# First attention of a two-block transformer kernel: the window branch's projection, key rotation and key spreading, and the compressed keys' rotation, at other units

## The reference, cut to what matters

```python
h = x @ w_in_even[li]
qa, ka, va, qn, kc, vc, ksl, vsl, kw, vw, g = _split(h, EVEN_SPLITS)
...
kc = partial_rope(compress(k_cmp, 0), cmp_end)   # branch 1: 15 compressed keys per group
...
ks = partial_rope(k_slc, pos)                    # branch 2: selected keys
...
kw_pad = jnp.pad(partial_rope(k_win, pos), ...)  # branch 3: window keys
...
return gb[..., 0:1] * o_c + gb[..., 1:2] * o_s + gb[..., 2:3] * o_w
```

## Time and profile before

| | |
|---|---|
| median of 3 runs | 1347.26 us (1346.98 to 1348.11) |
| the profiled execution | 1347.95 us |
| its span in the profile | 1346.2 us |
| TensorE busy | 1319.9 us, 98% of the span |
| VectorE busy | 681.1 us, 51% |
| ScalarE, GpSimd busy | 234.5 us and 95.6 us |
| mean granted TensorE clock | 0.997 of full speed |

### The profile page before, as it was taken

The page is one execution under the profiler, slowest core; times in us unless marked ns, Lnnn a source line. Parts: engine busy times, 40 slices in busy tenths (PEclk is TensorE's granted clock), DMA queues, the critical chain, the costliest instruction groups (busy, mean ns, idle before and its releaser), DMA issues.

```text
span 1346.2 us, 19454 instructions
## 1 busy us (share of the span) xinstructions
PE 1319.9 (98%) x7520; PEld 821.7 (61%) x7520; DVE 681.1 (51%) x1263; ACT 234.5 (17%) x547; POOL 95.6 (7%) x116
## 2 busy tenths in 40 slices
PE   9999999999999999999999999999999999999996
PEld 8667585786779557587687666644444444444433
DVE  1235588877889548977978254422122122212213
ACT  2134311111120341120122252100000000000002
POOL 1125400000011030000000100000000000000001
PEclk9999999999999999999999999999999999999999
DMA  9930154555514455577664504499999999999994
GB/s 380 360 142 34 64 220 177 219 228 218 185 67 157 183 194 201 217 270 280 233 240 168 187 34 186 180 420 421 421 420 416 422 421 421 422 421 421 421 420 194
DMA packets 51072, 359.56 MB, mean 267 GB/s; under 512 B 5920, under 2 KB 6192, under 8 KB 8496
## 3 DMA queue, kind: packets, MB, share of 16 engines
q1 hardware_dynamic: 45312, 324.60, 59.8%
q0 software_dynamic: 5392, 32.05, 6.5%
q10 hardware_dynamic: 288, 1.80, 0.3%
HBM read 356.88 MB, written 1.05 MB: 266 GB/s over the span
## 4 chain that ended last, share of the span: by engine, by line
PE 88%; DVE 8%; issue 1%; DMA 1%; ACT 0%; DVEq 0%; SPq 0%; ACTq 0%
PE ps L1536 13%; PE ps L1010 13%; PE ps L1001 9%; PE ps L1565 7%; PE ps L1461 7%; PE ps L1514 7%; PE ps L983 5%; PE ps L818 4%; PE ps L1291 4%; PE ps L901 2%; PE ps L1284 2%; PE ps L922 2%; DVE ring L2381 1%; DMA ring<-in_stream 1%; PE ps L823 1%
## 5 line engine op out<-in xcount | busy, mean ns | idle before, releaser
L2829 DVE TENSOR_TENSOR masked_and_probs<-ps,gate_rows 128x512 f32<-128x512 f32 x52 | 33.5, 686 | 152.4 <-PE ps L1565 152.4
L1514 PE MATMUL ps<-masked_and_probs,probT 128*128 128x512 f32 x208 | 94.4, 594 | 1.0 <-DVE masked_and_probs L2829 1.0
L1461 PE MATMUL ps<-masked_and_probs,mix_rows 128*128 128x256 f32 (+1 forms) x416 | 93.0, 376 | 0.0
L1461 PEld LDWEIGHTS ps<-masked_and_probs,mix_rows 128*128 128x128 f32 x416 | 75.0, 190 | 28.8 <-issue 19.6
L1001 PEld LDWEIGHTS ps<-xT,ring 128*128 128x128 f32 x768 | 87.8, 192 | 3.8 <-issue 3.8
L1001 PE MATMUL ps<-xT,ring 128*128 128x128 f32 x768 | 88.7, 275 | 0.0
L1010 PE MATMUL ps<-ring,qk_tiles 128*128 128x512 f32 x192 | 85.2, 592 | 0.0
L983 PE MATMUL ps<-ring,xT 128*128 128x512 f32 x192 | 83.8, 594 | 0.0
L2817 DVE TENSOR_TENSOR masked_and_probs<-masked_and_probs,ps 128x256 f32<-128x256 f32 x26 | 11.0, 421 | 142.0 <-ACT masked_and_probs L2003 142.0
L1673 ACT ACTIVATE qk_tiles<-ps 128x512 f32<-128x512 f32 (+7 forms) x58 | 30.1, 522 | 244.9 <-PE ps L1001 237.2
L1536 PE MATMUL ps<-ring,vec_rows 128*32 128x512 f32 (+2 forms) x296 | 72.0, 592 | 0.0
(11 more groups left out here) (500 smaller groups left out, 2379.9 us busy)
## 6 DMA issues: line engine op xcount, KB each, us to landing
ring<-in_stream SPq DMA_DIRECT2D x200, 1024.0 KB, 9.8
qk_tiles<-in_stream SPq DMA_DIRECT2D x46, 1024.0 KB, 20.0
v_rows<-in_ada POOLq DMA_DIRECT2D x12, 1024.0 KB, 5.2
qk_tiles<-in_ada POOLq DMA_DIRECT2D x12, 1024.0 KB, 5.2
vec_rows<-in_stream SPq DMA_DIRECT2D x12, 1024.0 KB, 17.0
con<-in_stream SPq DMA_DIRECT2D x12, 1024.0 KB, 18.6
y_rows<-in_stream SPq DMA_DIRECT2D x12, 1024.0 KB, 20.1
par<-in_stream SPq DMA_DIRECT2D x12, 1024.0 KB, 20.7
```

The lines of the kernel that those rows point to most:

```text
L1461: mm = pe.matmul(ps[:, 5 + kk // 2, kk % 2 * 2 * P:kk % 2 * 2 * P + width], h2[:, t, k * P:(k + 1) * P], select[:, t, 0:width], start=t == ...
L1514: mm = pe.matmul(ps[:, q, :], probT[:, buf, 256 + q // 2 * P:256 + (q // 2 + 1) * P], yslot[:, q % 2 * 512:(q % 2 + 1) * 512], start=False ...
L2829: dve.tensor_tensor(yslot[:, cols], ps[:, 5 + half, :], gaterow[:, 1, cols], ALU.mult).then_inc(ready, 1)
```

## The change

It moves work between units and reorders GpSimd's first steps; no instruction of work is added or removed.

- Compressed keys: TensorE's rotation from 4 to 3 (ahead of the query piece there), VectorE's from 5 to 4. The second half of the query pieces from 6, 7, 8, 9 to 5, 6, 7, 8.
- Queries: ScalarE's second copy from 10 to 9; VectorE's sine parts from 10 and 15 to 9 and 13.
- Branch 3: pieces from 14 to 19, 21, 22 to 11 to 18; ScalarE's copy from 23 to 19; VectorE's rotation from 27 to 24; spreading from 28 and 30 to 26 and 27.
- GpSimd: `spread_values` first, then a new wait for `s_ckey` 2, then `cosine_part(0)`.

```diff
--- before.py
+++ after.py
@@ -239,8 +239,8 @@
 
 
 STARTING = 4
-KEYS_AT = 5
-ROPE_AT = (10, 15)
+KEYS_AT = 4
+ROPE_AT = (9, 13)
 
 
 def by_scalar(u):
@@ -1230,12 +1230,12 @@
             pe.wait_ge(s_roped, 2)
             attention("a0", {
                 0: [compressed, lambda: queries(0, 0, 0)], 1: [lambda: queries(0, 0, 1)],
-                2: [lambda: queries(0, 1, 0), lambda: pe.wait_ge(s_projsb, 4)], 3: [lambda: queries(0, 1, 1)],
-                4: [rotate_compressed], 6: [lambda: queries(1, 0, 0)], 7: [lambda: queries(1, 0, 1)],
-                8: [lambda: queries(1, 1, 0)], 9: [lambda: queries(1, 1, 1)],
-                14: [lambda: window_keys(0)], 15: [lambda: window_keys(2)], 16: [lambda: window_keys(4)],
-                17: [lambda: window_keys(6)], 18: [lambda: window_values(0, 0)], 19: [lambda: window_values(0, 4)],
-                21: [lambda: window_values(1, 0)], 22: [lambda: window_values(1, 4)],
+                2: [lambda: queries(0, 1, 0), lambda: pe.wait_ge(s_projsb, 4)], 3: [rotate_compressed, lambda: queries(0, 1, 1)],
+                5: [lambda: queries(1, 0, 0)], 6: [lambda: queries(1, 0, 1)], 7: [lambda: queries(1, 1, 0)],
+                8: [lambda: queries(1, 1, 1)],
+                11: [lambda: window_keys(0)], 12: [lambda: window_keys(2)], 13: [lambda: window_keys(4)],
+                14: [lambda: window_keys(6)], 15: [lambda: window_values(0, 0)], 16: [lambda: window_values(0, 4)],
+                17: [lambda: window_values(1, 0)], 18: [lambda: window_values(1, 4)],
                 CMP_AT: [compressed_scores], CMP_AT + 8: [turn_compressed],
                 CMP_AT + 10: [lambda: compressed_sums(0)], CMP_AT + 11: [lambda: compressed_sums(1)]})
             out_projection(FIRST["out_even"], "mix0", lambda: turn_rows(x, "ln0", 0))
@@ -1839,10 +1839,10 @@
                 a, b = INSTANCES[name]
                 return {b - a + 1: lambda: take_turn(name.replace("a", "mix"), xT, only=0)}
 
-            exps("a0", {2: take_compressed, 4: lambda: take_queries(0), 10: lambda: take_queries(1), 23: take_window,
+            exps("a0", {2: take_compressed, 4: lambda: take_queries(0), 9: lambda: take_queries(1), 19: take_window,
                         24: exp_compressed, CMP_AT + 9: take_compressed_turn,
                         CMP_AT + 11: lambda: take_compressed_sums(0), CMP_AT + 12: lambda: take_compressed_sums(1)} | {
-                (5, 7, 28, 30)[2 * j + g]: (lambda j=j, g=g: spread_keys(j, g)) for j in range(2) for g in range(2)}
+                (5, 7, 26, 27)[2 * j + g]: (lambda j=j, g=g: spread_keys(j, g)) for j in range(2) for g in range(2)}
                 | turn_first_half("a0"))
             warm()
             take_turn("mix0", xT, only=1)
@@ -2164,7 +2164,7 @@
                     dve.tensor_scalar(drms, drms, -0.5, None, ALU.mult)
                     dve.tensor_scalar(drs.bitcast(I32), dnw.bitcast(I32), -1, ROOT_SEED, ALU.mult, ALU.add).then_inc(s_drs, 1)
 
-                return {DIFF_NORM_AT[0]: lambda: sums(0), DIFF_NORM_AT[1]: lambda: (sums(1), rope_keys(1)), DIFF_NORM_AT[1] + 1: first_guess}
+                return {DIFF_NORM_AT[0]: lambda: sums(0), DIFF_NORM_AT[1]: lambda: sums(1), DIFF_NORM_AT[1] + 1: first_guess}
 
             def branch_gates():
                 dve.wait_ge(s_expgate, 1)
@@ -2565,7 +2565,7 @@
 
             attention("a0", {2: branch_gates, KEYS_AT: rope_compressed, ROPE_AT[0]: lambda: rotated_queries(0),
                              ROPE_AT[1]: lambda: rotated_queries(1), CMP_AT + 1: compressed_masked, CMP_AT + 2: compressed_max,
-                             CMP_AT + 3: compressed_less_max, CMP_AT + 5: compressed_factors,
+                             CMP_AT + 3: compressed_less_max, CMP_AT + 4: lambda: rope_keys(1), CMP_AT + 5: compressed_factors,
                              CMP_AT + 6: compressed_weighed} | norm_diff() | turn_first_half("a0"))
             take_turn("mix0", xT, only=1)
             residual("out_even", 0, lambda t: layer_norm(t, vec[:, 0, :], vec[:, 2, :], s_vecA, 32), "ln0", 0)
@@ -3092,8 +3092,9 @@
                                    own[0:8 * NCMP, :].unsqueeze(2).to_broadcast([8 * NCMP, 8, HD]), ALU.mult
                                    ).then_inc(s_vspread, 1)
 
+            spread_values()
+            pool.wait_ge(s_ckey, 2)
             cosine_part(0)
-            spread_values()
             scale_group(0)
             roped_queries(0)
             cosine_part(1)
```

## The result

| | kernel before, run beside it | changed kernel |
|---|---|---|
| median of 22 runs | 1348.09 us (1346.93 to 1350.85) | 1350.55 us (1347.62 to 1352.22) |
| ratio of the two, 95% interval | | 1.0015 (1.0009 to 1.0020) |
| the profiled execution, its span | 1347.95, 1346.2 us | 1350.91, 1349.2 us |
| mean granted clock over the runs | 0.9969 (0.995 to 0.999), of the 35 beside e1 to e5 | 0.9936 (0.991 to 0.995) |

The change makes the kernel slower by about 0.15%, some 2 us. That is within the 0.2% called "no change" above, but a ratio of 1.0015 on 1347.26 is 1349.3: not 1.2 us sooner, and above the range's end of 1348.5.

What follows compares the result with a forecast made beforehand. TensorE, 88% of the last-ending chain, was taken as the bound, with VectorE bounding units 24 to 29. Terms 0.5 + 0.8 - 0.1 gave 1.2 us sooner: 1346.1 us against 1347.26, own range 1344.9 to 1347.5, with rivals 1344.0 to 1348.5.

Steps and rivals of the forecast that it cites:

- Part 1: Compressed keys one unit sooner, units 3 to 8: sums no longer overlap GpSimd's cosine product; 0.5 us won, bounds 0 to 0.8.
- Part 2: Query sine parts at units 9 and 13: removes the 0.45 us stall at unit 12; swapped rows land with 1.1 us margin.
- rival (d): Swapped rows of queries or keys take over 5 us, VectorE waits at 13 or 24, moves undo themselves; shared chance 0.12.
- Part 3 up to unit 20: Eight pieces moved to units 11 to 18: with earlier gains 1.3 us won, scores of 20 at 110.6; bounds 0.9 and 1.6.
- Part 3, units 20 to 29: Keys' rotation at unit 24, VectorE started sooner: 0.1 us lost by scores of 30; bounds 0.15 won, 1.8 lost.
- the walk: Step-by-step VectorE timing from scores of 20: rotation 5.7 to 6.84 us after them, scores of 30 at 12.55.
- the sum: At unit 30: 0.5 + 0.8 - 0.1 = 1.2 us sooner.
- Part 4: Spreading at units 26 and 27: exponential 28 delayed about 0.7 us, but covered, so no cost.
- I leave the clock's fall as it is: In the attention, the granted clock's fall was kept as before since thin TensorE stretches remain; no gain or loss counted.
- The prediction's own sign of being wrong: VectorE waiting before the keys' rotation, scores of 30 above 124.3, or two clock falls between 110 and 135.
- Rival (c): Units 22 to 28: thin stretch starts sooner, clock falls twice, another 1.6 us; 1347.7, or 1348.5 with late rows; chance 0.13.
- Rival (a): Units 24 to 28: idle time spread thinner, clock stays up, 1.6 us more won; 1344.5 us; chance 0.25.

Runs made afterwards that it cites:

- e1: Changed kernel with the third branch's pieces, copy, key rotation and spreading back where they were; ratio 0.9998 to the kernel before, 1348.30 us.
- e5: Changed kernel plus one spare 128-column product before the transposes of each of units 21 to 27; ratio 1.0027 to the kernel before, 1352.57 us.
- e17: Changed kernel with GpSimd's first steps in their old order and without the new wait; ratio 1.0018 to the kernel before, 1350.14 us.
- e8: Changed kernel plus three spare TensorE products, 512 columns in unit 25 and 256 in units 27 and 29; ratio 0.9987 to the kernel before, 1346.50 us.
- e12: Changed kernel with only ScalarE's spreading back at units 28 and 30; ratio 1.0019 to the kernel before, 1351.32 us.
- e3: Changed kernel with only the keys' rotation back at unit 27 and spreading at 28 and 30; ratio 0.9998 to the kernel before, 1348.62 us.
- e7: Kernel before with the change's whole third branch (pieces, copy, rotation, spreading) and nothing else of it; ratio 1.0025 to the kernel before, 1352.17 us.
- e14: Changed kernel plus spare products at units 25, 27 and 29, with GpSimd's old order and no new wait; ratio 1.0003 to the kernel before, 1348.67 us.
- e13: Changed kernel plus one spare 512-column product in unit 28, behind the turning of the compressed probabilities; ratio 1.0017 to the kernel before, 1350.17 us.
- e16: The kernel of e14 measured again on another chip; ratio 0.9997 to the kernel before, 1347.51 us.
- e15: The kernel of e8 measured again on another chip; ratio 0.9995 to the kernel before, 1347.22 us.

## Why the prediction was wrong

- **Part 1, right.** No stall at the moved query piece, 84.07 against 83.95 forecast, sums 0.19 each against 0.2. What was wrong is the reason beside it: the overlap with GpSimd goes because the sums come sooner (e17), and GpSimd's wait adds nothing. The Trainium skill, "SBUF — State Buffer", section on the two separate sides, has the two engines exclude one another. The traces agree: 1.41 against 0.38 for the sums; 1.24 for the second sine product, which started 0.69 before GpSimd's product beside it ended (100.25), and 0.74 for the first, which started 0.19 before (94.14).
- **Part 2, right in effect, its margin not.** Scores 12 start at 96.57 without a wait and with more work done; the second sine part had its rows at 99.56, and its 1.24 us lie under TensorE's pieces. But the rows were forecast to land 4.1 us after the first issue, with 1.1 us to spare. In e1, issued from 94.07, they were waited for until 99.22, 5.15 us after, which is the delay of rival (d). In the changed kernel, issued from 94.26, they would by that be there at 99.4 (an estimate), so the margin was about 0.2.
- **Part 3 up to unit 20, right.** Scores 20 at 110.67, forecast 110.6.
- **Part 3, units 20 to 29: the walk was nearly right, its reading not.** It had the rotation between masks 24 and 25 and mask 25 late, but it was summed only to scores 30, and no gap on TensorE was read off it on the way. The gap before scores 26 is 1.04, above the 0.86 that was the widest of before. With the clock up (e8) scores 30 come at 123.52, 0.37 later than the forecast 123.15; 0.28 of it is the subtraction, which takes 0.68 there too, beside GpSimd's product, where the walk had it as before. So up to unit 20 the moves won 1.30 and behind it they lost 0.44, not 0.1: 0.86 where the sum said 1.2. (The prediction's own range of 0.3 to 1.9 sooner also leaves out its lower bound for these units, 1.8 lost.)
- **Part 4, right.** e12, with the spreading back, is no faster.
- **The step that failed is "I leave the clock's fall as it is".** It took the fall, and its price of about 1.6 us, over from the kernel before, though the change moves VectorE's work ahead of scores 26. The runs showed in its place a fall that comes sooner and lasts longer: in the kernel before it began at 125.7, as the 512-column products came, and was over in 3.41 us, at a cost of 1.62; in the changed kernel it begins at 120.6, behind the gap that the rotation opens, and lasts until behind them, 10.24 us, at a cost of 4.14. That the rotation brings it is shown by e3, e7 and e12, and that the clock is the whole of the loss by e8; why it then lasts that long stays open. The prediction's own sign of being wrong came with it: scores 30 at 124.90, above 124.3. Rival (c) had the place (unit 22 to 28) and the sign, but a second fall of 1.6 as its shape; with one long fall at the measured 2.5 more than before, its sum would have been 2.5 - 1.2 = 1.3 us slower.
- **Rival (a) fell.** Its argument, that the idle time is spread thinner, is contradicted by the 1.04. The Trainium skill, "TensorE: Matmul & The Clock Gate", HAM oscillation, which asks only that there be no idle gaps of micros, would have given this rival; the clock fell behind gaps of 1.04 at most, and in e14 behind TensorE busy 6.00 of 6.00 us.

## What to carry to other kernels

A step put between two masks on VectorE can be free in the sum and still cost, by the gap that it opens on TensorE: follow the walk for its gaps, not only for its end. A fall of the clock has no fixed price; in this kernel it lasted from 3.41 to 10.24 us. A win seen in one unit can be gone a few units later (e1), so look where it ends up. Where the clock is near falling, time a change with the clock held up on both sides (here by three spare products) to learn what the moves themselves are worth, and compare the mean clock of many runs rather than one trace.

## What the runs showed of the hardware

- **The clock can stay down under nearly full work.** After its fall it stayed at the lower level (1.2 GHz) for 3.41, 6.83 or 10.24 us; in the changed kernel TensorE was busy 3.25 to 3.42 of each 3.41 us of it (as the profile models its busy time). It rose behind 512-column products in the changed kernel (10.24 us) and during one in e13 (6.83), and among products of 64 to 256 columns alone in e12 (6.83 and 10.24) and e5 (3.41). The Trainium skill, "TensorE: Matmul & The Clock Gate", What's actually happening, has sustained activity release the throttle; in the changed kernel nearly full work did not do so for 10 us.
- **It can fall without idle time.** In e14 it went down at about 114 behind 6.00 us without a gap. Ahead of it stand the products of `compressed_scores` (30 columns, 111.34 to 113.26) and seven of 64 or 128 columns. Whether those bring it on was not tried, and why it happened in some executions and not in others (e14 and e16 are one kernel) is open.
- **Spare products in the gaps held the clock.** Three of 512 and 256 columns, in the gaps before scores 26, 28 and 30, brought it from 0.9936 to 0.998 and 0.9963 (e8, e15). Products of 128 columns ahead of seven units' transposes, with the gap of 1.03 left open, gave 0.9932 (e5). The two differ in size, number and place, and no run tells which counts.
- **An operation of VectorE can take longer beside one of GpSimd.** The same subtraction took 0.40 us alone and 0.69 with 0.43 us of GpSimd's product still to run; the sums of the compressed keys 0.38 and 1.41. It goes the other way too: a product of GpSimd (L3058) that takes 0.61 alone took 0.94 when VectorE's sine product ran beside it.
